# Decoder layer on one core: the first FFN tile computed with seven block products instead of eight, interleaved with the second tile

## The reference

```python
n = rmsnorm(h, ln1_g);  proj = n @ w_in                      # 1024 -> 1536: pool | lru | gate
mix = concat(rmsnorm(pool_mixer(u_pool)), rmsnorm(rg_lru(conv(u_lru)) * gelu(u_gate)))
h = h + mix @ w_out
n2 = rmsnorm(h, ln2_g)
h = h + (silu(n2 @ w_ffn_gate) * (n2 @ w_ffn_up)) @ w_ffn_down   # D_FF = 2816
out = rmsnorm(h, lnf_g)
```

## Time and profile before

| | |
|---|---|
| median of three runs | 897.58 us |
| the profiled execution | 896.94 us |
| its span | 895.1 us |
| granted TensorE clock, mean | 0.999 |
| busy: PE / DVE / ACT / POOL | 882.8 / 614.1 / 394.4 / 274.0 us |

### The profile page before, as it was taken

How to read it: one execution, slowest core, us unless ns; L and a number is a source line. 1 busy time by engine, 2 the same in 40 slices (tenths; PEclk the granted TensorE clock), 3 DMA queues, 4 the chain that set the end, 5 groups by cost and what they waited for, 6 DMA issues and landing times.

```text
span 895.1 us, 11037 instructions
## 1 busy us (share of the span) xinstructions
PE 882.8 (99%) x3980; PEld 725.7 (81%) x3980; DVE 614.1 (69%) x848; ACT 394.4 (44%) x654; POOL 274.0 (31%) x209
## 2 busy tenths in 40 slices
PE   7999999999999999999999999999999999999997
PEld 6877788888888878888888888888888888888886
DVE  5778996655679757566565664756638975787667
ACT  6689733533665233332223323333234444454456
POOL 0000032733345465544555545455540000000000
PEclk9999999999999999999999999999999999999999
DMA  9033011132020333223332332333239933333324
GB/s 324 7 98 91 24 48 48 47 118 71 1 72 0 130 94 130 83 95 129 94 124 77 105 130 67 119 92 124 92 108 382 393 104 97 94 95 102 98 83 188
DMA packets 94318, 98.01 MB, mean 109 GB/s; under 512 B 5764, under 2 KB 63672, under 8 KB 94264
## 3 DMA queue, kind: packets, MB, share of 16 engines
q1 hardware_dynamic: 83736, 78.16, 26.0%
q10 hardware_dynamic: 10528, 19.15, 7.1%
HBM read 70.81 MB, written 24.38 MB: 106 GB/s over the span
## 4 chain that ended last, share of the span: by engine, by line
PE 97%; DVE 1%; DMA 1%; issue 0%; ACT 0%; POOL 0%; SPq 0%; DVEq 0%; ACTq 0%
PE bank L2105 23%; PE bank L2107 23%; PE bank L2106 23%; PE bank L1993 5%; PE bank L1994 5%; PE bank L1995 5%; PE bank L1937 3%; PE bank L1938 3%; PE bank L1939 3%; PE bank L2014 1%; PE bank L1971 1%; PE bank L1950 1%; DMA h<-in_x 0%; PE bank L1959 0%; DVE nT_lo L1301 0%
## 5 line engine op out<-in xcount | busy, mean ns | idle before, releaser
L721 POOL TENSOR_TENSOR r_lo<-gu_raw,r_hi 128x512 fp32r<-128x512 f32 x84 | 117.0, 1394 | 65.8 <-ACT r_hi L1021 65.7
L721 POOL TENSOR_TENSOR r_lo<-wsum_S,r_hi 128x512 fp32r<-128x512 f32 x63 | 97.9, 1553 | 127.6 <-ACT r_hi L1021 127.6
L2105 PE MATMUL bank<-T_hi,r_lo 128*128 128x512 f32 x336 | 130.7, 389 | 0.0
L2106 PE MATMUL bank<-T_lo,r_hi 128*128 128x512 f32 x336 | 130.7, 389 | 0.0
L2107 PE MATMUL bank<-T_hi,r_hi 128*128 128x512 f32 x336 | 130.7, 389 | 0.0
L2106 PE MATMUL bank<-d_lo,h_hi 128*128 128x512 f32 (+1 forms) x312 | 120.5, 386 | 0.0
L2107 PE MATMUL bank<-d_hi,h_hi 128*128 128x512 f32 (+1 forms) x312 | 120.5, 386 | 0.0
L2105 PE MATMUL bank<-d_hi,h_lo 128*128 128x512 f32 (+1 forms) x312 | 120.5, 386 | 0.0
L1021 ACT CAST r_hi<-gu_raw 128x512 fp32r<-128x512 f32 x84 | 52.2, 621 | 126.3 <-PE bank L2107 126.3
L2105 PE MATMUL bank<-nT_hi,r_lo 128*128 128x512 f32 x252 | 98.1, 389 | 0.6 <-POOL r_lo L721 0.6
L2107 PE MATMUL bank<-nT_hi,r_hi 128*128 128x512 f32 x252 | 98.0, 389 | 0.0
...
## 6 DMA issues: line engine op xcount, KB each, us to landing
...
gu_raw<-in_w_ffn_gate SPq DMA_DIRECT2D x22, 512.0 KB, 3.7
gu_raw<-in_w_ffn_up SPq DMA_DIRECT2D x22, 512.0 KB, 4.8
...
w_raw<-in_w_in SPq DMA_DIRECT2D x11, 512.0 KB, 4.1
h<-in_x SPq DMA_DIRECT2D x8, 512.0 KB, 6.5
```

Of the source, the lines that this page charges most:

```text
L721: pool.tensor_tensor(lo_of(n)[:], a_block(f, name), f32(hi_of(n)[:]), ALU.subtract)\
L2105: pe.matmul(bank, s_lo, m_hi, start=(opens and j == 0), stop=False, skip_group_check=True)
L2106: pe.matmul(bank, s_hi, m_lo, start=False, stop=False, skip_group_check=True)
```

## The change

- Tile 0 also takes Strassen's seven products. They alternate with those of tile 1: M1 of both, M2 of both, M3, M6, M7, M5, M4 of both, 14 products in all. M3 has moved ahead of M6, in a bank of its own. `transposes(14)` now stands before the first product, `transposes(15)` after the second.
- The weight sums of both tiles are made earlier, in the token loop (m = 3 to 6), in buffers of their own. The up weights of tile 1 are loaded at 206 us instead of 255 us.
- The block B12 enters no product any more except inside the T sums, which read `raw`. Its hi and lo parts are no longer made: four casts on ACT fall away. For m = 4 to 7 POOL now makes the lo part of B22 (`nT_lo_c`) instead of B12's, and DVE makes none.
- The stores of A11 and A12 count on semaphores of their own. silu into a block waits for that block's store and for the sums that read it, not for all seven stores. The 11 loads of the down weights' block 21 share one semaphore.
- Two pieces of a lo part of the output weights and the scratch tile for squares have moved to other places in memory.

Order of DVE's instructions where the T sums are made, before. `raw` holds the token blocks, `T_lo` the lo parts, `hid` tile 0's results, `wsum_S` and `gu_raw` tile 1's weight sums.

The core of the diff (new buffers, counts and the renamed helpers are left out):

```diff
-        M7_BANK = 7
-        SECOND = ("M1", "M2", "M6", "M7", "M5", "M4", "M3")
-
-        def products(f):
-            return SECOND if f == 1 else PRODUCTS
+        FIRST = ("M1", "M2", "M3", "M6", "M7", "M5", "M4")
         def entry(f, pr):
-            return 4 + 7 * (f - 1) + products(f).index(pr)
-
-        NE = 4 + 7 * (FT - 1)
-
+            return 2 * FIRST.index(pr) + f if f < 2 else 7 * f + PRODUCTS.index(pr)
+
+        NE = 7 * FT
         def gu_count(f):
             return 32 * (f // 2 + 1) - 16 * (f % 2)
-        ENTRIES = [(0, a) for a in ("A11", "A12", "A21", "A22")] \
-            + [(f, A_OF[pr]) for f in range(1, FT) for pr in products(f)]
+        ENTRIES = [(f, A_OF[pr]) for pr in FIRST for f in range(2)] \
+            + [(f, A_OF[pr]) for f in range(2, FT) for pr in PRODUCTS]
...
         def chain_bank(f, c):
-            return psum[(4 if f == 1 else 3 * (f % 2)) + c]
+            return psum[(4, 2, 6)[c] + f] if f < 2 else psum[3 * (f % 2) + c]
         def product_bank(f, pr):
-            return psum[M7_BANK] if f == 1 and pr in ("M7", "M4") else chain_bank(f, CHAIN[pr])
+            return psum[f] if f < 2 and pr == "M3" else chain_bank(f, CHAIN[pr])
...
-                put(p, "A11", hid[0][0][:])
-                put(p, "A12", hid[1][0][:])
+                put(p, "A11", hid[0][0][:], hid_a11_out)
+                put(p, "A12", hid[1][0][:], hid_a12_out)
...
+            def nT_lo_c(m):
+                pool.wait_ge(raw_ok, 2 * m + 2)
+                pool.wait_ge(n_hi_ok, norm_hi_count(m, 1))
+                pool.tensor_tensor(nT_lo[:, KH:KT, cols(m)], raw[1][:, :, cols(m)], f32(nT_hi[:, KH:KT, cols(m)]),
+                                   ALU.subtract).then_inc(nlo_c_ok, 1)
...
-                nT_lo_a(m)
+                if m < 4:
+                    nT_lo_a(m)
+                else:
+                    nT_lo_c(m)
...
-                    act.copy(nT_hi[:, 4 * b:4 * b + 4, cols(n % TT)],
-                             bank[:].rearrange("p (k n) -> p k n", k=4)).then_inc(n_hi_ok, 1)
+                    if n - TT < 4 or b == 1:
+                        act.copy(nT_hi[:, 4 * b:4 * b + 4, cols(n % TT)],
+                                 bank[:].rearrange("p (k n) -> p k n", k=4)).then_inc(n_hi_ok, 1)
...
-                if p > 0:
-                    act.wait_ge(hid_out, 16 * 7 * p)
-                act.activation(hid[f % 2][0][:], src_[:], ACT.Silu).then_inc(silu1_ok, 1)
+                act.wait_ge(ent_ok, done(entry(f, "M2")))
+                if f == 1:
+                    act.wait_ge(r_lo_ok, entry(1, "M3") + 1)
+                if p > 0 and f % 2 == 0:
+                    act.wait_ge(hsum_ok, 4 * (p - 1) + 3)
+                    act.wait_ge(hid_a11_out, 16 * p)
+                if p > 0 and f % 2 == 1:
+                    act.wait_ge(hsum_ok, 4 * p)
+                    act.wait_ge(hid_a12_out, 16 * p)
+                act.activation(hid[f % 2][0][:], chain_bank(f, 0)[:], ACT.Silu).then_inc(silu1_ok, 1)
...
+            copy_m1(0)
+            copy_m1(1)
+            nT_hi_part(2 * TT - 1)
             hi_entry(5)
+            t_hi("T2", 0)
+            hi_entry(6)
             silu1(0)
-            t_hi("T2", 0)
             t_hi("T2", 1)
             t_hi("T3", 0)
             t_hi("T3", 1)
-            hi_entry(6)
-            silu2(0)
-            copy_m1(1)
+            silu1(1)
+            hi_entry(7)
             t_hi("T1", 0)
             t_hi("T1", 1)
-            hi_entry(7)
-            hi_entry(8)
+            for n in range(8, 12):
+                hi_entry(n)
             t_hi("T4", 0)
             t_hi("T4", 1)
+            hi_entry(12)
+            hi_entry(13)
+            hi_entry(14)
+            silu2(0)
+            hi_entry(15)
+            silu2(1)
+            hi_entry(16)
+            hi_entry(17)
...
-                if m >= 2:
+                if 2 <= m < 6:
                     nT_lo_b(m - 2)
                 if m < TT:
                     second_variance(m)
+                if m in (3, 5):
+                    weight_sums(m // 4, ("S1",))
+                if m in (4, 6):
+                    weight_sums(m // 6, ("S4",))
                 if m == TT:
                     t_sums(0)
...
+            def gate_second(f):
+                dst = hid[f % 2][1][:]
+                dve.wait_ge(u2_ok, f + 1)
+                if f < 2:
+                    dve.wait_ge(ent_ok, done(entry(f, "M5")))
+                    step(dve.tensor_tensor(dst, chain_bank(f, 2)[:], u2(f)[:], ALU.add))
+                    dve.tensor_tensor(dst, product_bank(f, "M3")[:], dst, ALU.add).then_inc(c12_ok, 1)
+                else:
+                    dve.wait_ge(ent_ok, done(entry(f, "M3")))
+                    dve.wait_ge(hid_out, 16 * 5 * (f // 2))
+                    dve.tensor_tensor(dst, chain_bank(f, 2)[:], u2(f)[:], ALU.add).then_inc(c12_ok, 1)
+
+            t_sums(1)
+            t4_sums()
+            for name, g in T_HI[0:6]:
+                t_lo(name, g)
+            second_sum(0)
+            second_sum(1)
+            for name, g in T_HI[6:]:
+                t_lo(name, g)
+            third_sum(0)
+            third_sum(1)
+            up_second(0)
+            gate_second(0)
+            weight_sums(2, ("S1",))
+            up_second(1)
+            gate_second(1)
+            hidden2(0)
+            up_first(0)
+            hidden1(0)
+            weight_sums(2, ("S4",))
+            up_first(1)
+            hidden1(1)
+            hidden2(1)
...
-            for t in range(2):
-                if t == 1:
-                    gate_up_product(1, "M1")
-                pe.wait_ge(op_evac, 4 * TT - 2 + 2 * t)
-                pe.wait_ge(nlo_a_ok, 4 * (t + 1))
-                pe.wait_ge(nlo_b_ok, 4 * (t + 1))
-                for w in range(2):
-                    for kh in range(2):
-                        n = 2 * w + kh
-                        if t == 0:
-                            pe.wait_ge(r_lo_ok, n + 1)
-                            if n == 1:
-                                transposes(2 * TT - 2, xs2)
-                            if n == 3:
-                                transposes(2 * TT - 1, xs2)
-                        ins = product(psum[2 * t + w][:], [(*weight_tile(n, k), *b_block(f"B{kh + 1}{t + 1}", k))
-                                                           for k in range(KH)], kh == 0, kh == 1)
-                        if t == 1:
-                            ins.then_inc(ent_ok, 1)
-                    if t == 0:
-                        ins.then_inc(f0_ok, 1)
-            for f in range(1, FT):
-                for pr in products(f):
-                    if (f, pr) != (1, "M1"):
-                        gate_up_product(f, pr)
+                        closes(f, pr)).then_inc(ent_ok, 1)
+
+
+
+            transposes(2 * TT - 2, xs2)
+            gate_up_product(0, "M1")
+            gate_up_product(1, "M1")
+            transposes(2 * TT - 1, xs2)
+            for pr in FIRST[1:]:
+                for f in range(2):
+                    gate_up_product(f, pr)
+            for f in range(2, FT):
+                for pr in PRODUCTS:
+                    gate_up_product(f, pr)
```

More of the change, by code:

```diff
@@ L106, in hymba_pool_rglru_block @@
         wo_hi[2] = wo_hi[0]
-        wo_lo3 = [at("wo_lo3_0", 192.25, [P, 2, 512], F32R), at("wo_lo3_1", 108, [P, 2, 512], F32R)]
+        wo_lo3 = at("wo_lo3", 192.25, [P, 2, 512], F32R)
+        wo_lo3_end = [at(f"wo_lo3_end{k}", 66 + 8 * k, [P, 512], F32R) for k in range(2)]
         y0_lo = at("y0_lo", 152.25, [P, GT, S], F32R)
@@ L1047, in second_half_squares @@
                                accum_out=ssq[:, TT + m:TT + m + 1]).then_inc(sq_ok, 1)
-            for m in range(TT + 2):
+            for m in range(TT + 1):
                 if m < TT:
@@ L1642, in second_variance, with weight_sums @@
                     .then_inc(var_ok, 1)
-            for m in range(TT + 2):
+            def weight_sums(f, names):
+                g = gu_raw[f % 2]
+                a11, a12, a21, a22 = g[:, 0, 0:KH], g[:, 0, KH:KT], g[:, 1, 0:KH], g[:, 1, KH:KT]
+                sums = wsum(f)
+                if "S1" in names:
+                    if f == 1:
+                        dve.wait_ge(gate_1_in, 16)
+                    dve.wait_ge(gu_in[f % 2], gu_count(f))
+                    if f >= 2:
+                        dve.wait_ge(r_lo_ok, entry(f - 1, "M5") + 1)
+                    dve.tensor_tensor(sums["S1"][:], a21, a22, ALU.add).then_inc(wsum_ok, 1)
+                    dve.tensor_tensor(a21, a11, a21, ALU.subtract).then_inc(wsum_ok, 1)
+                    dve.wait_ge(wsum_ok, wsum_count(f, "S1"))
+                    dve.tensor_tensor(sums["S2"][:], sums["S1"][:], a11, ALU.subtract).then_inc(wsum_ok, 1)
+                if "S4" in names:
+                    if f >= 2:
+                        dve.wait_ge(r_lo_ok, entry(f - 1, "M3") + 1)
+                    dve.wait_ge(wsum_ok, wsum_count(f, "S2"))
```

(15 more changed lines are left out.)

289 lines of the change are left out of this document (125 added, 164 removed).

## The result

| | before | after |
|---|---|---|
| median | 896.86 us (896.80 to 897.67, 6 runs) | 904.10 us (902.41 to 906.23, 6 runs) |
| ratio | | 1.0078, 95% interval 1.0068 to 1.0088: slower by 0.8% |
| the profiled execution | 896.94 us | 906.23 us |
| its span, granted clock | 895.1 us, 0.999 | 904.4 us, 0.993 |

The forecast was 901.0 us, in a range of 895.0 to 904.5 us. The 896.86 us is also the lowest of the medians that before had in five comparisons; the others are 897.41 to 897.75 us, and against them after is 6.4 to 6.7 us slower and not 7.2.

What follows compares the result with a forecast made beforehand. PE's own instruction list was taken to bound the kernel. -2.72 - 0.78 + 3.8 + 3.2 = +3.5 us on the profiled 896.94 us gave 900.4 us, and 901.0 us for the median; range 895.0 to 904.5 us.

Steps and rivals of the forecast that it cites:

- the 3.5 us of gain: On PE's path: one product fewer, -2.72 us, and the stall at 313.55 us removed, -0.78 us.
- the case that had a chance of 0.16 (the clock down): POOL passed over by DVE, or PE's clock down: 902 to 905 us, chance 0.16.
- the one that had 0.5: Forecast with both new waits, at M6 and M7 of tile 0: 899.5 to 902.5 us, chance 0.5.
- One product, one stall: Tiles 0 and 1 have 14 products instead of 15, -2.72 us; PE's stall at 313.55 us goes, -0.78 us.
- Weight sums in the token loop, costed at 0: Eight DVE weight sums before the FFN, hidden in DVE's idle time: 0; otherwise under 1 us lost per pass, twice.
- First gap, 3.8 us: PE at M6 of tile 0 waits for T2: start at 276.6 instead of 272.8 us, 3.8 us.
- 11.9 + 4.4 = 16.3 us: Between last xs and first M6: DVE's own work, 11.9 us, plus four POOL rows taking turns with it, 4.4 us.
- Second gap, 3.2 us: PE at M7 of tile 0 waits for u2, behind T3's and T1's lo parts: 285.2 against 282.0 us, 3.2 us.
- if it gets one turn more: Ahead of M7 of tile 0, POOL getting one more turn than assumed makes the second wait 4.2 us.
- passed over: Rival: POOL's entry of the first M6 waits for eight DVE rows; 8.2 us of waits, 902.2 us; chance 0.16 with clock down.
- Full gain: Rival: T sums are through by 272.8 us and nothing waits, 894.1 us; full or nearly full gain, chance 0.16.
- The clock falls in the gap: Rival: the 3.8 us gap lowers PE's clock, up to +2.3 us, 903 us; chance 0.16 with POOL passed over.

Runs made afterwards that it cites:

- e1: Kernel after with four of POOL's lo parts before the first M6 cut to 8 of 128 columns, some lo terms left out: 899.95 us, ratio 1.0023.
- e3: Kernel after with u2 of tile 0 moved on DVE ahead of T1's lo parts: 900.31 us, ratio 1.0030.
- e8: Kernel after with POOL's four lo parts cut to 8 columns and u2 of tile 0 ahead of T1's lo parts: 896.25 us, ratio 0.9983.
- e2: Kernel before with only the finer semaphores of the stores and the shared one of block 21's loads: 896.97 us, ratio 0.9993.
- e6: Kernel after with the transposes of token tile 6 moved behind M1 of tile 0: 903.04 us, ratio 1.0064.
- e4: Kernel after with 12 extra matmuls that feed nothing just before the wait at M7 of tile 0: 903.05 us, ratio 1.0066.
- e12: Kernel after with matmuls that feed nothing in both gaps, ten before M6 and 13 before M7 of tile 0: 903.95 us, ratio 1.0071.
- e5: Kernel after with M5 of both tiles ahead of M6 and T1's lo parts ahead of T4's sums: 902.19 us, ratio 1.0051.

## Why the prediction held, and where it didn't

- *Direction and mechanism.* Right. DVE and POOL take turns, T2 is late for M6 of tile 0, u2 is late for M7, and the 3.5 us of gain is overrun. e1, e3 and e8 show each cause by itself. The size is not: +7.2 us is twice the +3.4 forecast, and 904.1 us lies near the top of the range, in the case that had a chance of 0.16 (the clock down), not in the one that had 0.5. That the range held it is in part luck.
- *One product, one stall: -2.72 and -0.78.* Right. 12 matmuls are gone; the wait near 313 us is gone, and e2 shows it going by itself. The forecast had nothing late behind M7, though, and the pause at 321.17 us costs 0.4 us.
- *Weight sums in the token loop, costed at 0.* This step failed in its trace: PE waits 1.2 us for an `xs`. I had counted the sums against DVE's idle time and priced the miss at "under 1 us, twice". I didn't add up what stands ahead of an `xs` in a pass: the three S1 sums take 3.0 us with one POOL row over them, and a POOL row also holds the short rows. In the kernel's time PE's wait hardly counts, as e6 shows, since it shortens the first gap by the same amount.
- *First gap, 3.8 us.* It was 3.1, and 4.4 with the 1.3 us at `xs`, which the forecast had in no other place. From the first T sum to the second T2 piece I had 11.9 + 4.4 = 16.3 us; the rows give 278.5 - 262.45 = 16.05. The price of a POOL row, 1.1 us, was 1.04 in e1. What failed is the starting point, that the last `xs` ends at the same time in either kernel. It ends at 262.53 us instead of 260.31; 1.2 us of that is the program's start, and 1.0 us comes, as I read DVE's rows, from the `xs` ahead of it, which the sums of the token loop make late. Against those, PE itself was 1.6 us later at M6 than the forecast has it with the start taken off. The `rstd` product of 128x1 ahead of the last `xs`, held for 1.23 us in after, is no part of the difference, since the profile of before has it too:

```profile
257.78 1.22 DVE L1274 TENSOR_TENSOR rstd<-rstd,tmp 128x1 f32<-128x1 f32 x1
```

- *Second gap, 3.2 us.* It was 4.0. The prediction gave 4.2 us "if it gets one turn more", and POOL did: besides its row at 277.92 and the two from 280.34, the first of the two from 284.10 also stands ahead of u2. Each of the four T3 and T1 pieces lasts about 2.3 us.
- *Sum.* Forecast +3.4 us on the median, measured +7.2. The measured terms at the full clock are -2.7 - 0.8 + 1.3 + 3.1 + 4.0 + 0.4 = +5.3. e4 and e12, where no low clock is left on the path, lie at +5.5 and +6.4 us. The rest, 0.8 to 1.7 us, holds the clock's part and the low median of before in after's comparison (896.86 us, where e4's and e12's have 897.58 and 897.53), and the runs bound it but don't split it.
- *Rivals.* POOL was never passed over: each of its rows waited for at most one of DVE's. "Full gain" was wrong by the same POOL rows it named. "The clock falls in the gap" came true, and was no rival to the two waits but an addition to them. I had let the fall happen at the first gap, with part of it hidden; in the profiled run it fell at the second, where nothing hides it.

The Trainium skill's "SBUF — State Buffer", section "SBUF: two separate sides", has the lock held for a whole instruction by whichever engine starts first. e1 agrees, at 1.04 us for a row. The Trainium skill's "TensorE: Matmul & The Clock Gate", in its closing table, warns of idle gaps between bursts of matmuls. The traces agree that the clock can fall by them, to 0.50 with PE's wait of 3.8 us at M7 in after. In the profiles with shorter waits the outcome differs: it stayed at 1.00 with one of 2.8 us in e1 and of 3.0 us in after, and fell with one of 2.7 us in e5, of 2.9 us in e3 and of 3.0 us in e4.
